# Hybrid attention, delta rule and expert block on Trainium2: GpSimd products ahead of the substitution, a reordered scan, weight loads per slot

## What is computed

```python
def chunked_gated_delta_rule(q, k, v, g, beta):
    g = jnp.cumsum(chunks(g), axis=-1)
    decay = jnp.exp(jnp.where(tri, g[..., :, None] - g[..., None, :], -jnp.inf))
    k_beta = k * beta[..., None]
    lower = jnp.where(tri_strict, einsum('bhncd,bhnsd->bhncs', k_beta, k) * decay, 0.0)
    rhs = concatenate([v * beta[..., None], k_beta * jnp.exp(g)[..., None]], axis=-1)
    sol = triangular_solve(lower + eye, rhs, left_side=True, lower=True, unit_diagonal=True)
    u, w = sol[..., :Dv], sol[..., Dv:]
    def step(state, xs):
        q_c, k_c, u_c, w_c, intra_c, gl_c = xs
        v_new = u_c - einsum('bhck,bhkv->bhcv', w_c, state)
        o_c = einsum('bhck,bhkv->bhcv', q_c, state) + einsum('bhcs,bhsv->bhcv', intra_c, v_new)
        state = state * jnp.exp(gl_c)[..., None, None] + einsum('bhck,bhcv->bhkv', k_c, v_new)
        return state, o_c
h = h + concat(A, B) @ w_out
h = h + MoE(RMSNorm(h))      # top 4 of 32 experts
```

## Time and profile before

| what | value |
|---|---|
| median of 3 runs (lowest, highest) | 1371.28 us (1369.92, 1372.37) |
| the profiled execution's own time | 1371.59 us |
| its span in the profile | 1369.8 us |
| mean granted TensorE clock | 0.943 |
| busy: PE, DVE, ACT, POOL | 88%, 37%, 15%, 21% |
| DMA: moved, mean | 446.55 MB, 326 GB/s |

### The profile page before, as it was taken

How to read it: one execution, slowest core, us unless ns; L and a number is a source line. 1 busy time by engine, 2 the same in 40 slices (tenths; PEclk the granted TensorE clock), 3 DMA queues, 4 the chain that set the end, 5 groups by cost and what they waited for, 6 DMA issues and landing times.

```text
span 1369.8 us, 30476 instructions
## 1 busy us (share of the span) xinstructions
PE 1210.8 (88%) x12030; PEld 566.0 (41%) x12031; DVE 504.8 (37%) x1213; ACT 206.3 (15%) x415; POOL 283.8 (21%) x381
## 2 busy tenths in 40 slices
PE   7989997989889887979798899988989777799896
PEld 6865554766533332324233333333333222233333
DVE  1236857455333332323233233323333223233332
ACT  4135662133000000000000000000000000000000
POOL 1000004000122222223122223222222222222222
PEclk9999999899799999989899999999999988999999
DMA  6221140439789999999999999999999999998991
GB/s 204 64 67 62 31 123 8 152 147 397 312 346 415 418 419 415 417 419 416 416 417 419 399 381 395 406 403 417 417 421 418 416 421 419 421 415 353 421 408 27
DMA packets 67696, 446.55 MB, mean 326 GB/s; under 512 B 17008, under 2 KB 37688, under 8 KB 43088
## 3 DMA queue, kind: packets, MB, share of 16 engines
q1 hardware_dynamic: 48736, 424.97, 75.1%
q0 software_dynamic: 16176, 18.91, 6.1%
q10 hardware_dynamic: 2752, 2.23, 0.5%
HBM read 435.37 MB, written 15.07 MB: 329 GB/s over the span
## 4 chain that ended last, share of the span: by engine, by line
DMA 46%; PE 37%; DVE 7%; issue 5%; ACT 1%; POOL 1%; SPq 1%; DVEq 1%; POOLq 1%; ACTq 0%
DMA XG<-hn_scratch,IDXC 22%; DMA BDN<-in_expert_b_down 21%; PE PS L636 17%; PE PS L1001 12%; PE PS L1014 4%; DMA out<-Y,IDXS 3%; PE PSC L636 2%; DVE XT L1377 2%; POOL IDXC L391 1%; DVE GU L1386 1%; DMA W<-in_w_in 1%; SPq L208 1%; DVEq L1423 0%; DVE W L1230 0%; DVE W L1231 0%
## 5 line engine op out<-in xcount | busy, mean ns | idle before, releaser
L1001 PE MATMUL PS<-W,XT 128*32 128x512 f32 x5184 | 608.6, 623 | 116.4 <-DVE XT L1377 107.1
L1001 PEld LDWEIGHTS PS<-W,XT 128*32 128x32 f32 x5184 | 169.3, 114 | 516.5 <-issue 409.0
L1014 PE MATMUL PS<-W,AT 128*32 128x256 f32 x5184 | 294.6, 379 | 1.2 <-DVE AT L1397 1.2
L636 PE MATMUL PS<-W 128*128 128x512 f32 (+7 forms) x898 | 250.2, 439 | 10.4 <-DVE W L1175 7.5
L1014 PEld LDWEIGHTS PS<-W,AT 128*32 128x32 f32 x5184 | 169.5, 110 | 145.8 <-issue 47.8
L636 PEld LDWEIGHTS PS<-W 128*128 128x128 f32 (+1 forms) x898 | 151.8, 195 | 95.0 <-issue 75.3
L1386 DVE TENSOR_TENSOR GU<-PS,BGU 128x512 f32<-128x512 f32 x81 | 56.0, 692 | 363.1 <-PE PS L1001 360.4
L409 POOL DMA_INDIRECT out<-Y,IDXS x81 | 130.4, 1610 | 103.5 <-ACT Y L625 96.7
L625 ACT ACTIVATE Y<-SIG,ident 128x256 f32<-128x256 f32 x81 | 41.2, 508 | 656.1 <-DMA out<-Y,IDXS 629.5
L394 POOL DMA_INDIRECT XG<-hn_scratch,IDXC x82 | 87.3, 1064 | 73.4 <-POOL IDXC L391 69.3
L405 POOL COPY IDXS<-IDX 128x1 uint32 (+1 forms) x81 | 14.8, 183 | 391.9 <-DMA out<-Y,IDXS 391.8
(11 more groups left out here) (254 smaller groups left out, 539.9 us busy)
## 6 DMA issues: line engine op xcount, KB each, us to landing
W<-in_expert_w_gate_up SPq DMA_DIRECT2D x128, 2048.0 KB
W<-in_expert_w_down SPq DMA_DIRECT2D x64, 2048.0 KB
W<-in_w_in SPq DMA_DIRECT2D x10, 1024.0 KB, 5.3
W<-in_x SPq DMA_DIRECT2D x8, 512.0 KB, 10.2
W<-in_w_out SPq DMA_DIRECT2D x2, 1024.0 KB, 9.7
W<-in_w_out SPq DMA_DIRECT2D x1, 2048.0 KB, 8.2
hn_scratch<-W POOLq DMA_DIRECT2D x4, 512.0 KB, 11.1
out<-W ACTq DMA_DIRECT2D x4, 512.0 KB, 11.0
```

Source lines behind the costliest of these rows:

```text
L636: return pe.matmul(o, l, r, start=st, stop=sp_)
L1001: last = pe.matmul(GPS[32 * j:32 * j + 32, :].rearrange("p (g n) -> p g n", g=2), XT[:, 32 * k:32 * k + 32], rhs, start=(k == 0), stop=(k ...
L1014: last = pe.matmul(DPS[32 * j:32 * j + 32, :], AT[:, 32 * k:32 * k + 32], DNW[p][:, k, j * QW:(j + 1) * QW], start=(k == 0), stop=(k == KD ...
```

## The change

- **GpSimd.** `QET` of chunk 2 and `CT` of chunks 0 and 1 are made ahead of the clearing, `QET` of chunk 3 and `CT` of 2 and 3 behind it. The clearing waits for the last sigmoid product (`silu`), no longer for `st_ps`; the transposes to `U` on DVE wait for that. `KBEG` and `KTE` are made by ScalarE, one instruction for each head.
- **ScalarE** sends its four corner copies ahead of the last scaled values (`corners_out`).
- **PE and DVE.** Of the attention units, 0 to 4 stay ahead of the block steps, unit 5 is cut into four pieces inside the second level, unit 6 into four pieces in the scan, and unit 7 stands behind the scan. The additions move with them. The first scan step takes `USOL` itself instead of a copy of it. The output from the state is issued before the state update, the output from the values after it.
- **SP.** `WO1`, the router's weights and biases are loaded while the substitution runs. The gate-up slots of expert 0 each have their own wait.
- **Tiles.** `QET` of chunk 3 and the second state move out of the slots that are loaded early.

The diff, cut to its core:

```diff
-                  QET=slot(W1, 18944 + 512 * c) if c < 3 else slot(W0, 15360), T=slot(W0, 512 * c), U=slot(W0, 2048 + 512 * c),
+                  QET=slot(W1, 18944 + 512 * c) if c < 3 else slot(W0, 20736), T=slot(W0, 512 * c), U=slot(W0, 2048 + 512 * c),
-        STATES = [STATE, B[0]["T"]]
+        STATES = [STATE, slot(W0, 24016)]
...
             sp.dma_start(SYS, sys_d).then_inc(S_("sys_moved"), 16)
+            sp.wait_ge(S_("li"), 2 * NT)
+            sp.wait_ge(S_("qet"), NT)
+            sp.dma_start(WO1, w_out[512:1024, :].rearrange("(k p) n -> p k n", p=P)).then_inc(S_("wo_in"), 16)
+            sp.dma_start(RW, router_w.rearrange("(k p) n -> p k n", p=P)).then_inc(S_("res_in"), 16)
+            sp.dma_start(RB, rep(router_b)).then_inc(S_("res_in"), 16)
+            sp.dma_start(FWT, norm_ffn_w.rearrange("(k p) -> p k", p=P), allow_slow_non_contiguous=True).then_inc(S_("res_in"), 16)
             sp.wait_ge(S_("sys_done"), 1)
             sp.dma_start(inv_d, SYT).then_inc(S_("sys_moved"), 16)
...
+            sp.wait_ge(S_("sys_moved"), 16 * 18)
+            gu_part(0, 0, [3])
+            sp.wait_ge(S_("bias_zeros"), 4)
+            biases(0, 0)
             sp.wait_ge(S_("att_proj"), 2 * NT)
             dn_part(0, 0, [0])
-            sp.wait_ge(S_("bias_zeros"), 4)
-            biases(0, 0)
+            sp.wait_ge(S_("uw_ps"), 2 * NT)
+            gu_part(0, 0, [0])
+            sp.wait_ge(S_("kv_ps"), NT - 1)
+            gu_part(0, 0, [1])
+            sp.wait_ge(S_("vnew"), NT - 1)
+            sp.wait_ge(S_("o_ps"), 1)
+            gu_part(0, 0, [2])
             sp.wait_ge(S_("o_ps"), NT)
-            gu_part(0, 0, range(4))
...
             q_decayed(0)
             q_decayed(1)
-            g.wait_ge(S_("st_ps"), 8)
+            q_decayed(2)
+            corner_masked(0)
+            corner_masked(1)
             g.wait_ge(S_("proj_ps"), TOKU + CHU)
+            g.wait_ge(S_("silu"), CHU)
             for b in B:
                 g.memset(b["T"], 0.0).then_inc(S_("t_zero"), 1)
...
-            q_decayed(2)
             q_decayed(3)
-            for c in range(NT):
-                g.tensor_tensor(h4(B[c]["CT"]), h4(B[c]["LT"]), bm(MSK, HD), ALU.mult).then_inc(S_("ct"), 1)
-            for c in range(NT):
-                g.tensor_tensor(h4(B[c]["KBEG"]), h4(B[c]["KA"]), bc(EG[:, 4 * c:4 * c + 4], P), ALU.mult).then_inc(S_("k_scaled"), 1)
-            for c in range(NT - 1):
-                g.tensor_tensor(h4(B[c]["KTE"]), h4(B[c]["KA"]), bc(EGD[:, 4 * c:4 * c + 4], P), ALU.mult).then_inc(S_("k_scaled"), 1)
+            corner_masked(2)
+            corner_masked(3)
...
+                if i == CHU + 1:
+                    corners_out()
                 if 10 <= i:
                     hd = i - 10
...
+            for key, factor, count in (("KBEG", EG, NT), ("KTE", EGD, NT - 1)):
+                for c in range(count):
+                    for h in range(HD):
+                        hs = slice(h * P, (h + 1) * P)
+                        ins = a.activation(B[c][key][:, hs], B[c]["KA"][:, hs], ACT.Copy, scale=factor[:, 4 * c + h:4 * c + h + 1])
+                    ins.then_inc(S_("k_scaled"), 1)
...
-            for n in range(1, 2 * NT):
+            for n in range(1, 5):
                 att_unit(n)
...
+                if NT <= m < 2 * NT:
+                    att_unit(5, [m - NT])
...
+            uw(0)
+            pe.wait_ge(S_("u_upd"), STEPS)
+            state_update(0)
+            uw(1)
+            from_values(0)
+            uw(2)
+            correction(1)
+            from_state(1)
+            att_unit(6, [0])
+            state_update(1)
+            from_values(1)
+            uw(3)
+            correction(2)
+            from_state(2)
+            att_unit(6, [1])
+            state_update(2)
+            from_values(2)
+            att_unit(6, [2])
+            correction(3)
+            from_state(3)
+            att_unit(6, [3])
+            pe.wait_ge(S_("vnew"), NT - 1)
+            from_values(3)
+            att_unit(7)
...
+            new_values(3)
+            out_normed(0)
+            out_squares(1)
+            att_add(6)
+            out_normed(1)
+            out_squares(2)
+            att_add(7)
+            out_normed(2)
+            out_squares(3)
+            out_normed(3)
```

199 lines of the change are left out of this document (106 added, 93 removed).

## The result

The changed kernel takes **1355.3 us** (median of 4 runs, 1352.5 to 1360.8) beside 1370.6 us for the kernel before on the same chip (1369.5 to 1372.4): a ratio of 0.989, 95% interval 0.9875 to 0.9907. In a later measurement it took 1354.2 beside 1371.8 us, ratio 0.989 (0.9859 to 0.9918). It is faster by 1.1%. The prediction was 1357 us, in a range of 1351 to 1364.

The account below looks back on a forecast made before the run. DMA paces the expert loop, whose end follows its start, so gains in the delta rule ahead count fully. 17.4 - 2.5 - 3.6 = 11.3 us, with half the clock's 5.8 us 14.2; 1371.3 - 14.2 = 1357 us, range 1351 to 1364.

Parts of the forecast that it names:

- clock does not fall: Rival, chance 0.23: TensorE keeps its full clock through steps and scan, so the gain is 17.1 us, giving 1354 us.
- GpSimd ahead of the substitution: GpSimd finishes before the substitution, so 11 of DVE's instructions there take 0.24 instead of 1.05 us: 8.9 us saved.
- The products moved ahead do not hinder the convolution: GpSimd products moved beside the convolution cost VectorE 0, bound 2.5 us; the rival with that loss had chance 0.20.
- Corners, 3.4 us: ScalarE sends its corner copies earlier, so the read-back ahead of the substitution goes out at 217.1 instead of 220.55.
- Steps, 17.4 us in all: Block steps start at 233.4 instead of 250.79, containing the 8.9 and 3.4 us; the other 5.1 is units taken off.
- Unit 5 in the steps, -2.5 us: Its four pieces add 3.44 us of PE to the block steps, of which 0.96 us idle time hides part.
- Scan, 0 for its order; 21.2 us at the full clock: From first product to last new values: 21.2 us against the old order's 21.1 at full clock, so no gain.
- Tail, -3.6 us: From the last new values to the first output unit: 7.6 us instead of 4.0, through VectorE's normings and ScalarE's root and copy.
- Weight loads, 0: Expert loads ahead of the loop: one slot early and four at the scan's end in both kernels; bounds 0 and +5 us.
- Clock, half of 5.8 us: Low clock cost 1.5 us in the steps and 4.3 in the scan's first products; half was taken as regained.
- The slower rival: Chance 0.03: PE's wait and the small tiles put the clock down through the output projection; 1384.5 us.
- The loop's end follows its start: Expert loop: what the delta rule gains before 297 us reaches the end one for one, if weights already in SBUF stay the same.

Follow-up runs that it names:

- e1: The kernel before with only the changed kernel's GpSimd order and ScalarE scalings; 1362.6 us, ratio 0.9926.
- e2: The changed kernel with the seven key scalings (KBEG, KTE) back on GpSimd behind its other products; 1367.1 us, ratio 0.9976.
- e3: The changed kernel with all eight attention units ahead of the block steps, scan in its new order without units; 1362.9 us, ratio 0.994.
- e11: e9 with the routing stage's idle transposes replaced by 2, 3 and 11 idle matmul calls, sized to the gaps; 1352.8 us, ratio 0.9872.
- e4: The changed kernel with the down slot's load behind the gate and up slots on SP's queue; 1358.0 us, ratio 0.9904.
- e7: The changed kernel with PE's wait ahead of the steps filled with 16 transposes of 128x128; 1353.7 us, ratio 0.9864.
- e9: e6 and e5 together, with ScalarE's copy of the transposed group moved ahead of a square root; 1352.3 us, ratio 0.9863.
- e8: e2 with 14 idle matmul calls behind the fourth attention unit, filling PE's wait ahead of the steps; 1363.6 us, ratio 0.9948.
- e5: The changed kernel with the first transposition group of the output issued ahead of unit 7 on PE; 1356.9 us, ratio 0.9905.
- e6: The changed kernel with PE's wait ahead of the steps filled with two idle matmul calls; 1353.5 us, ratio 0.987.
- e10: e9 with the routing stage's idle transposes replaced by 4, 6 and 36 idle matmul calls; 1355.3 us, ratio 0.9893.

## Why the prediction was right, and which of its terms were off

The time came as forecast, with the case "clock does not fall" for the profiled execution; of the two medians, 1355.3 lies between that case and the forecast, and 1354.2 on the case.

Part of that is luck. In no trace did the half of the clock's term happen that the forecast of 1357 rests on. And in the profiled pair two things cancel that are no part of the sum: the rounds ended 2.4 us later and the loop was 2.7 us shorter. Laid on the attention addition, the first output unit comes 18.9 us earlier, where the sum with the full clock had 17.1; the terms below make up the 1.8 us.

*GpSimd ahead of the substitution, 8.9 us.* Measured 9.0 (17.4 to 8.4 us), and 9.0 again by itself in e1. The Trainium skill ("SBUF — State Buffer", who interferes with whom) has an exclusive lock for the ports that both engines share. The rows of e2 agree: 0.97 us beside GpSimd's products, 0.21 behind them, while the addition with a PSUM operand takes 0.69 us in all traces. The products moved ahead do not hinder the convolution (cost 0): with the first projection group at 3.72 us as before, the addition behind the rounds stands at 216.31 (e3) and 216.90 (e11), and stood at 217.06. What the prediction left out is the clock in the units behind that wait, 1.8 us before the change (see e1).

*Corners, 3.4 us.* The read-back went out at 219.17, 3.8 us earlier when both traces are laid on the attention addition. e3 adds what the prediction did not say: the term counts only because units leave the path as well (steps 24.2 us after the addition with it and without).

*Steps, 17.4 us in all.* Measured 17.8 from the addition, with PE waiting 1.70 us for the inverse (forecast 2).

*Unit 5 in the steps, -2.5 us.* They grew from 16.74 to 17.60 us, by 0.9. With the 1.5 us that the clock gave back, the forecast's net is 1.0.

*Scan, 0 for its order; 21.2 us at the full clock.* Measured 20.8, with PE never waiting, beside the 21.1 that the old order was put at. The 0 holds for order and pieces together. In e3 the order alone gains some 2.4 us up to the last values, and in the changed kernel the three pieces of unit 6 (2.6 us) take their place.

*Tail, -3.6 us.* Measured -2.8: 6.8 us in place of 7.6. The chain is the one that was summed, with hand-overs shorter than put.

*Weight loads, 0.* The bunch came behind unit 7, as said, and e4 shows that nothing hangs on it.

*Clock, half of 5.8 us: this is the step that failed.* I took half because the rows could not tell whether it would fall. In both traces of the changed kernel it does not fall ahead of the output projection, which gives 1354.2 us by the prediction's own sum (17.1); 1352.5 and 1352.4 were measured.

Why it does not fall is not shown by an experiment of its own, but the record points at the pieces of unit 5, the prediction's own argument for that case. Without them (before, e1, e3) the clock fell in each trace, 11 to 12 us into the steps, though wide matmuls without a wait stood ahead. With them it stayed up in all nine traces in which PE waited 2.0 us or less ahead of the steps (the changed kernel twice, e4 to e7, e9 to e11), and in e8 behind its bridge. These kernels differ in the wait and in unit 6 too, so a kernel that differs in the pieces alone is still to be tried.

The medians lie higher than the traces, by some longer executions. Of the 21 executions of kernels with the wait unfilled (the changed kernel twice, e4, e5; 1.7 to 2.0 us in their traces), 8 took over 1357 us, the bound that e6's expectation had set, at mean clocks of 0.943 to 0.949. Of the 17 with it filled (e6, e7, e9, e11), none did. Were the wait of no account, the 8 would all fall among the 21 in 0.4% of cases. On the one chip that ran both kinds at the same time (e4 to e7) it is 6 of 11 against none of 9, 1.2%. Together with e2 and e8 this points to the wait ahead of the steps as what makes the long executions. It is not shown: no long execution of the changed kernel left a trace, the 17 are of four kernels, and a low mean clock alone does not make an execution long (1351.8 us at 0.949 in e7).

The Trainium skill ("TensorE: Matmul & The Clock Gate", what's actually happening) ties the level to how busy the engine was. For the fall in e2 this holds: it came inside PE's wait, and filling the wait kept the clock up. For the falls before, in e1 and in e3 it does not hold if busy is read as in the profile (PE busy for 15.78 of the steps' 16.74 us in all three), nor for the return, since PE was busy for all 31.14 us of e2's steps at 0.50.

*The slower rival (chance 0.03)* did not come: the longest of the changed kernel's ten executions took 1366.0 us. But its mechanism, a wait and then small tiles that stay at the lower level, is real in this very place: e2 lengthens the wait from 1.7 to 3.1 us and pays 13.5 us in the steps of its trace. The argument against it, that PE had idled before and the clock had come back, looked at wide matmuls as what follows the wait.

*"The loop's end follows its start"* holds for the change as a whole (18.7 us at its first gather, 21.0 at its last), but not for a shift of the loop's start alone: e10 starts 8 to 10 us late and loses 3. (e11 starts 1.7 us early and shows no gain, but so little is within what the loop varies by.) The loads of the second expert's slots stand on the output projection's progress and not on the loop's start, and the change moved both. That would explain it, but it was not tried by itself.
